# Gate and up products of the feed-forward layers with both parts of x as one moving operand of 512 columns

## What is computed

```python
def swiglu(h, w_gate, w_up, w_down):
    return (jax.nn.silu(h @ w_gate) * (h @ w_up)) @ w_down
...
    for i in range(DEPTH):
        mod = (c_act @ mod_w[i] + mod_b[i]).reshape(B, N_SUBLAYERS, 3, D)
        shift, scale, gate = mod[:, :, 0], mod[:, :, 1], mod[:, :, 2]
        h = modulate(rms_norm(x, norm_g[i, 0]), shift[:, 0], scale[:, 0])
        x = x + MACARON_WEIGHT * gate[:, 0, None, :] * swiglu(h, ffn_w_gate[i, 0], ffn_w_up[i, 0], ffn_w_down[i, 0])
        ...
        x = x + gate[:, 1, None, :] * y
        h = modulate(rms_norm(x, norm_g[i, 2]), shift[:, 2], scale[:, 2])
        x = x + MACARON_WEIGHT * gate[:, 2, None, :] * swiglu(h, ffn_w_gate[i, 1], ffn_w_up[i, 1], ffn_w_down[i, 1])
```

## Time and profile before

| | |
|---|---|
| time, median of 3 runs (lowest to highest) | 2218.18 us (2216.0 to 2218.39) |
| the profiled execution's own time | 2219.53 us |
| its span, first to last instruction | 2218.2 us |
| mean granted TensorE clock | 0.988 of full speed |
| PE busy | 2140.0 us, 96% of the span |
| DVE busy | 1497.4 us, 68% |
| ACT busy | 1082.5 us, 49% |
| GpSimd busy | 156.6 us, 7% |

### The profile page before, as it was taken

One profiled execution on the slowest core, in us unless ns is written; L12 is line 12 of the kernel. 1 busy time (PEld: TensorE's weight loads), 2 busy tenths in 40 slices (PEclk: granted clock), 3 DMA queues, 4 the chain that ended last, 5 costly groups with the idle time before them and its releaser, 6 DMA issues.

```text
span 2218.2 us, 33120 instructions
## 1 busy us (share of the span) xinstructions
PE 2140.0 (96%) x14096; PEld 1889.0 (85%) x14096; DVE 1497.4 (68%) x1960; ACT 1082.5 (49%) x1217; POOL 156.6 (7%) x192
## 2 busy tenths in 40 slices
PE   7999998999999999899999999999999999999998
PEld 5998765998899878687799887897998878988996
DVE  4677676877777786576655455568786655677874
ACT  4443565543444354555544346644554457444652
POOL 0311110111011100000000011100000111000000
PEclk9999998999999999999999999999999999999999
DMA  9977662987787855244355564435655564446651
GB/s 347 307 267 263 249 244 86 302 279 271 249 273 257 288 210 182 88 171 152 115 191 189 190 226 169 171 124 166 217 178 194 194 211 153 136 152 209 190 176 53
DMA packets 262818, 448.61 MB, mean 202 GB/s; under 512 B 11616, under 2 KB 147104, under 8 KB 262416
## 3 DMA queue, kind: packets, MB, share of 16 engines
q1 hardware_dynamic: 243616, 376.64, 50.2%
q0 software_dynamic: 18768, 68.75, 8.8%
q10 hardware_dynamic: 288, 1.11, 0.1%
HBM read 445.40 MB, written 1.06 MB: 201 GB/s over the span
## 4 chain that ended last, share of the span: by engine, by line
PE 88%; ACT 5%; DVE 5%; issue 1%; DMA 0%; SPq 0%; ACTq 0%; DVEq 0%
PE ps L1522 86%; ACT whi L1747 2%; DVE wlo L1952 1%; PE ps L1713 1%; PE ps L1680 1%; ACT S L1747 1%; ACT L1747 1%; ACT xhi L1747 1%; ACT xs L1747 0%; DVE S L2100 0%; DMA raw<-in_mod_w 0%; PE ps L1670 0%; DVE nbuf L2060 0%; ACT PT L1747 0%; PE ps L1630 0%
## 5 line engine op out<-in xcount | busy, mean ns | idle before, releaser
L1952 DVE TENSOR_TENSOR wlo<-raw,whi 128x2048 fp32r<-128x2048 f32 (+1 forms) x339 | 767.2, 2271 | 349.8 <-ACT whi L1747 349.3
L1747 ACT ACTIVATE whi<-raw 128x2048 fp32r<-128x2048 f32 (+1 forms) x339 | 640.7, 1895 | 363.6 <-PE ps L1522 343.7
L1522 PE MATMUL ps<-xhi,whi 128*128 128x256 f32 x2632 | 649.8, 287 | 6.4 <-DVE wlo L1952 4.4
L1522 PE MATMUL ps<-xhi,wlo 128*128 128x256 f32 x2632 | 643.5, 284 | 0.0
L1522 PEld LDWEIGHTS ps<-xhi,whi 128*128 128x128 f32 x2632 | 507.9, 193 | 11.7 <-issue 7.2
L1522 PEld LDWEIGHTS ps<-xhi,wlo 128*128 128x128 f32 x2632 | 508.0, 193 | 2.3 <-issue 2.0
L1522 PE MATMUL ps<-xlo,whi 128*128 128x256 f32 x2632 | 344.3, 283 | 0.1
L1522 PEld LDWEIGHTS ps<-xlo,whi 128*128 128x128 f32 x2632 | 327.6, 192 | 0.5 <-DVE xlo L2066 0.3
L1522 PE MATMUL ps<-whi,xhi 128*128 128x512 f32 x736 | 296.7, 403 | 13.5 <-DVE wlo L1952 10.5
L1522 PE MATMUL ps<-wlo,xhi 128*128 128x512 f32 x736 | 290.4, 395 | 0.0
L1522 PE MATMUL ps<-whi,hhi 128*128 128x512 f32 x528 | 210.0, 398 | 0.0
(11 more groups left out here) (234 smaller groups left out, 1966.7 us busy)
## 6 DMA issues: line engine op xcount, KB each, us to landing
raw<-in_w_in SPq DMA_DIRECT2D x52, 1024.0 KB, 4.9
raw<-in_ffn_w_gate SPq DMA_DIRECT2D x88, 512.0 KB, 4.6
raw<-in_ffn_w_up SPq DMA_DIRECT2D x88, 512.0 KB, 6.0
raw<-in_ffn_w_down SPq DMA_DIRECT2D x44, 1024.0 KB, 5.0
raw<-in_w_up SPq DMA_DIRECT2D x88, 512.0 KB, 4.8
raw<-in_dil_w_in SPq DMA_DIRECT2D x36, 1024.0 KB, 5.1
xs<-in_mod_w POOLq DMA_DIRECT2D x54, 512.0 KB, 6.2
nbuf<-in_mod_w POOLq DMA_DIRECT2D x46, 512.0 KB, 5.2
```

The lines of the kernel that those rows point to most:

```text
L1522: return nc.tensor.matmul(o, lhs, rhs, start=start, stop=stop, skip_group_check=True)
L1747: return nc.scalar.activation(o, i, func, **kw)
L1952: V.tensor_tensor(wlo[:, s["c"], 0:s["n"]], raw[:, s["slot"], 0:s["n"]], whi[:, s["c"], 0:s["n"]].bitcast(F32), ALU.subtract).then_inc(sem ...
```

## The change

Units 3 to 10 of each of the four layers (32 units of 44) are made in another form. `xhi` and `xlo` become two halves of one tile (`xhl` in the trace), so that one matmul can take both as a moving operand of 512 columns: `whi` by high x lands in the left half of a bank, `whi` by low x in the right half. `wlo` by high x stays a matmul of 256 columns into the left half. A unit has four output blocks, so it needs four banks; even units take G0 to G3, odd ones D0 to D3. Nothing on PE adds the halves any more. ACT copies the right halves to `e1` and `e2`, DVE adds the left halves from PSUM (two sums), ACT takes silu of `e1` in place, DVE multiplies, and the rest is as before. The turns of the modulation come between a unit's two pieces instead of behind the second, and take their bank from the four that the unit doesn't use.

```diff
-    def feature(self, src, need, nk=NC):
+    def feature(self, src, need, nk=NC, mid_turns=False):
...
+            if mid_turns and k0 == 0:
+                self.run_turns()
         self.x_read = tok
-        self.run_turns()
+        if not mid_turns:
+            self.run_turns()
...
     def gateup(self, q):
-        self.gateup_out(q, *self.feature("x", self.need_x))
+        if q < 3:
+            self.gateup_out(q, *self.feature("x", self.need_x, mid_turns=q == 2))
+        else:
+            self.gateup_wide(q)
+
+    def gateup_wide(self, q):
+
+        banks, self.idle_bank = ((G0, G1, G2, G3), D3) if q % 2 == 0 else ((D0, D1, D2, D3), G3)
+        bank_free = [self.free[b] for b in banks]
+        for k0 in (0, 4):
+            pc = self.take()
+            tok = self.ev("pe", "piece")
+            self.add("wide", banks=banks, k0=k0, c=pc["c"], w_lo=pc["w_lo"], need=[self.need_x(k0 + kk) for kk in range(4)],
+                     bank_free=bank_free if k0 == 0 else [])
+            self.used(pc, tok)
+            self.run_work()
+            if k0 == 0:
+                self.run_turns()
+        self.x_read = tok
+        s = q % 2
+        low = [self.ev("act", "low_out") for _ in range(2)]
+        gate = self.ev("dve", "wide_sum")
+        act = self.ev("act", "gate_act")
+        up = self.ev("dve", "wide_sum")
+        td = self.ev("dve", "hidden")
+        self.add("gateup_wide", s=s, banks=banks, piece=tok, e_free=self.e_free[s], low_out=low, gate=gate, gate_act=act, up=up)
+        self.free[banks[0]] = self.free[banks[1]] = gate
+        self.free[banks[2]] = self.free[banks[3]] = up
+        self.hidden_split(q, s, 1, td)
...
+                elif k == "wide":
...
+                        for m in range(4):
+                            w, v = vh[:, kk, m * P:(m + 1) * P], vl[:, kk, m * P:(m + 1) * P]
+                            mm(ps[:, s["banks"][m], :], w, xboth[:, :, kc, :], kc == 0, kc == NC - 1)
+                            ins = mm(ps[:, s["banks"][m], 0:T], v, xhi[:, kc, :], False, kc == NC - 1)
+                    ins.then_inc(sem["piece"])
...
+                elif k == "gateup_wide":
+                    q.wait_ge(s["piece"])
+                    q.wait_ge(s["e_free"])
+                    for e, b in ((e1, s["banks"][0]), (e2, s["banks"][2])):
+                        act(e[:, s["s"], :].rearrange("p (b n) -> p b n", b=2), ps[:, b:b + 2, T:2 * T],
+                            ACT.Copy).then_inc(sem["low_out"])
+                    q.wait_ge(s["gate"])
+                    act(e1[:, s["s"], :], e1[:, s["s"], :], ACT.Silu).then_inc(sem["gate_act"])
...
+                elif k == "gateup_wide":
+                    for e, b, low, n in ((e1, s["banks"][0], s["low_out"][0], 0), (e2, s["banks"][2], s["low_out"][1], 1)):
+                        q.wait_ge(low)
+                        o = e[:, s["s"], :].rearrange("p (b n) -> p b n", b=2)
+                        V.tensor_tensor(o, o, ps[:, b:b + 2, 0:T], ALU.add).then_inc(sem["wide_sum"])
+                    q.wait_ge(s["gate_act"])
+                    q.wait_ge(s["up"])
+                    V.tensor_tensor(e2[:, s["s"], :], e1[:, s["s"], :], e2[:, s["s"], :], ALU.mult).then_inc(sem["hidden"])
```

More of the change, by code:

```diff
@@ L32 @@
     "square", "moment", "var", "sqrt", "recip", "scaled", "x_turned", "x_hi", "x_full", "x_lo", "gate_mul", "resid",
-    "half", "gate_act", "hidden", "h_hi", "h_lo", "score", "biased", "expd", "weighed",
+    "half", "low_out", "wide_sum", "gate_act", "hidden", "h_hi", "h_lo", "score", "biased", "expd", "weighed",
     "turned", "pt", "value", "o_hi", "o_lo", "kept", "hn_sq", "hn_sum", "hn_sqrt", "hn_rec", "hn_mul", "hn_out",
@@ L73, in __init__ @@
         self.in_down = False
+        self.idle_bank = D3
         self.mod_ready = {}
@@ L310, in mod_part @@
             self.acc_turns.append([age or (2 if self.in_down else 1),
-                                   lambda: self.mod_turn(i, u, (G3 if self.in_down else D3) - u % 2, tok, acc)])
+                                   lambda: self.mod_turn(i, u, (G3 if self.in_down else self.idle_bank) - u % 2, tok, acc)])
     def mod_turn(self, i, u, bank, row, acc=None):
@@ L469, in down @@
             self.run_turns(age=False)
-            self.in_down = True
+            self.in_down, self.idle_bank = True, D3
             bank_free = [self.free[b] for b in (D0, D1, D2, D3)]
@@ L1363, in build @@
         nbuf = named("nbuf", [P, 4, T])
-        xhi = named("xhi", [P, NC, T], F32R)
-        xlo = named("xlo", [P, NC, T], F32R)
+        xboth = named("xhl", [P, 2, NC, T], F32R)
+        xhi, xlo = xboth[:, 0, :, :], xboth[:, 1, :, :]
         ident = named("ident", [P, P])
@@ L1560, in pe_program @@
                             ins = mm(place(m), vh[:, kk, m * P:(m + 1) * P], al[:, kc, :], False, kc == s["nk"] - 1)
+                    ins.then_inc(sem["piece"])
+                elif k == "wide":
+                    for t in s["bank_free"]:
+                        q.wait_ge(t)
+                    q.wait_ge(s["w_lo"])
+                    vh, vl = weights(s["c"], 4, 512)
+                    for kk in range(4):
+                        kc = s["k0"] + kk
+                        q.wait_ge(s["need"][kk][0])
+                        q.wait_ge(s["need"][kk][1])
+                        for m in range(4):
+                            w, v = vh[:, kk, m * P:(m + 1) * P], vl[:, kk, m * P:(m + 1) * P]
+                            mm(ps[:, s["banks"][m], :], w, xboth[:, :, kc, :], kc == 0, kc == NC - 1)
+                            ins = mm(ps[:, s["banks"][m], 0:T], v, xhi[:, kc, :], False, kc == NC - 1)
                     ins.then_inc(sem["piece"])
```

## The result

The changed kernel takes 2222.76 us (median of 20 runs, 2215.69 to 2227.84), the kernel before 2216.76 us in 20 runs of its own (2214.04 to 2221.57). The ratio is 1.0023, with a 95% interval of 1.0015 to 1.0031: about 5 us slower (3.3 to 6.9), at the edge of the 0.2% that the prediction calls no change. The runs of the change spread over 12.2 us, those of before over 7.5 us, and a longer run is mostly one with a lower clock: the four longest (2224.96 to 2227.84 us) have a mean granted clock of 0.984 to 0.987, the four shortest (2215.69 to 2219.07) one of 0.988 to 0.990.

A forecast was written before the change was run, and what follows sets the result against it. PE was taken to bound the kernel, with DVE's chain setting the pace in A to C after the change: 1.8 + 1.1 + 1.5 - 3.4 = +1.0 us, execution 2220.5 us, less 1.35 us for the median: 2219.2 us, range 2210 to 2225.5.

The forecast's parts named there:

- the prediction's own case: Wide units go at DVE's pace in layers A to C and PE's in D; 2214 to 2222 us, chance 0.52.
- within 0.2%: Whole kernel: no change a measurement can tell, under about 4.4 us either way; chance 0.57.
- PE's unit, 11.09 us: Wide feed-forward unit on PE: 32 x 0.2267 + 32 x 0.120 = 11.09 us, against 11.52 us before.
- That term of the sum: Layer D, without modulation parts, stays at PE's pace and keeps 8 x 0.43 = 3.4 us.
- DVE's round, 12.07 us: DVE's chain through one wide unit in layers with parts: 10.68 us grows by 1.39 us to 12.07 us.
- From unit 7 or 9 on PE goes at DVE's pace.: Wide units of A to C: DVE falls behind about 1 us a unit until PE must wait for it.
- The limit of 2.2 us: Wide units: DVE's lag at which PE first waits, for the bank a turn's result leaves 8.3 us into the round.
- The down phase is kept: First `wlo` behind the last sum to the last part's end stays as before: 48.38 us in C, 47.60 us in B.
- About 3 us at the last turn of A, B, C.: PE waits about 3 us for its last part at the last turn of each of these layers.
- The sum for A: Layer A, taken as the mean of B (1.1 us) and C (1.8 us): 1.5 us longer.
- The clock: Rival: the granted clock falls behind PE's waits at the last turns of A to C, 5.2 us, 2224.4 us; chance 0.13.
- three signs of being wrong: Down phase shorter by 2 us or more, late wide units' first sums under 11.8 us apart, or clock falling at last turns.

The follow-up runs named there:

- d_only: Wide form only in layer D, A to C narrow as in the kernel before: 2216.64 us, ratio 0.9994 to before.
- abc_only: Wide form only in layers A, B and C, D narrow as in the kernel before: 2224.37 us, ratio 1.0025 to before.
- contiguous: The changed kernel with the two parts of x side by side, so the 512 moving columns are one run of memory: 2223.24 us, ratio 1.0022 to before.

## Why the prediction was right in its number and wrong in a part

The prediction was 2219.2 us in a range of 2210.0 to 2225.5, and the measured median, 2222.76, lies inside. It lies outside the 2214 to 2222 us of the prediction's own case, and against before the forecast was +1.0 us where the ratio gives +5.1. The likeliest outcome was "within 0.2%" (0.57); it came out at that border, on the slower side, and the interval of the ratio doesn't tell which side of the border it is.

- **PE's unit, 11.09 us.** Right for seven of the thirteen units of A to C that have no turn; five take 11.31 us, and one in A, with a wait, 12.02. In D all take 11.31 us, so D keeps 1.7 us and not 3.4. That term of the sum was too large by 1.7 us. I took 0.2267 us from matmuls outside these layers; those of the down phase, in the same trace, start 0.233 us apart and give 11.31.
- **DVE's round, 12.07 us.** The step to the first `wlo` is 4.57 us (483.07 to 487.64), against 4.59. But two parts were charged with their busy time of 1.53 us, while the next instruction starts 1.45 us behind, twice a round. Over the seven rounds of layer C, first parts and results of turns included, the mean is 12.02 us (637.36 to 721.51), where the forecast's terms give 12.22. Late rounds are 11.6 and 12.5 us in turn.
- **"From unit 7 or 9 on PE goes at DVE's pace."** This failed. PE waits 0.65 us once in A, and nowhere over 0.15 us in the wide units of B and C. It finished unit 10 of C 92.59 us behind unit 2, against 95.61 us before, and had the whole gain in hand. Units with a turn take 12.0 us, so the lag grows more slowly than against 11.09 us. The limit of 2.2 us was wrong too: it is 11.09 - 8.3 us, less the usual 0.63, but the unit in question is the one with the turn. With 12.0 us the limit is 3.1 us, less what taking the result needs (0.15 to 0.7 us). In B and C the first sums in front of a unit with a turn come at most 3.1 us behind their unit's end, 2.5 beyond 0.63, and PE doesn't wait. In A they come 3.6 us behind it, at 129.48 us, and here it does (rows of DVE, then of PE):

```profile
136.27 1.53 DVE L2036 SCALAR_TENSOR_TENSOR xs<-nbuf,csil,xs 128x512 f32<-128x512 f32 x2
137.72 0.68 DVE L2044 TENSOR_TENSOR rows<-ps,rows 128x512 f32<-128x512 f32 x1
...
138.46 0.50 PE L1554 MATMUL ps<-xhl,whi 128*128 128x512 f32 x1 [0.65 <-DVE rows L2044]
```

- **The down phase is kept.** Right within what it varies. From the first `wlo` behind the last sum to the end of the last part: 49.0, 46.6 and 47.8 us in A, B and C, against 47.3, 47.6 and 48.4 us before. In `d_only`, whose A to C are in the order of before, it is 48.6, 49.1 and 49.6 us, so I carried over as fixed a term that differs by over 1 us between executions. With all kernels that keep the unchanged order it is 46.6 to 49.7 us.
- **"About 3 us at the last turn of A, B, C."** Right on the mean: nine waits in three executions of the wide form (the change, `abc_only`, `contiguous`) have a mean of 2.8 us.
- **The sum for A.** Wrong. I gave A the mean of B and C. But A has one turn fewer before the end of its unit 10, so before the change DVE entered its down phase 98.56 us behind unit 2 there and 99.43 us in B. With the change it is 101.31, 100.28 and 100.66 us in A, B and C: 2.7, 0.9 and 1.2 us later. The last turn starts 2.1, -0.5 and +0.4 us later than before, as means of the three executions, +2.0 us in all, where I had +4.4.
- **The clock.** This was a rival with 0.13, and it is the larger part of what is lost. Over the three executions the clock falls behind six of nine last turns. Counted from the start of the turn, since a lower clock costs nothing while PE waits, the time at the lower level takes 1.7, 6.1 and 4.5 us of PE's work, 4.1 us on the mean; the rival's price was 5.2 us. Its condition, two of the three waits, was met in two of the three executions and not in the change's own. The step that failed is its chance: I set one wait of 1.8 us with the clock at 1.00 against one of 1.9 us with 0.57 and took the fall for the exception. The sum with what was measured is 2.0 + 4.1 - 1.7 = 4.4 us. The layers' lengths in the three executions give +4.5 us as their mean, and the ratio 5.1.

Two of the prediction's three signs of being wrong showed: the clock fell at the last turns, and first sums of late wide units lay less than 11.8 us apart in every second round (697.40 to 709.02), though not on the mean. The errors had opposite signs: DVE's lag cost 2.4 us less than forecast, D gave 1.7 us less, and the clock took 4.1 us that my own case left out. That the range held is owed to the rivals in it and in part to luck; it doesn't make the likeliest case right.

## What to carry to other kernels

An engine that is busy 81% of a stage can still be the late one, if each of its rounds waits for another engine's answer; put work that depends on nothing into those waits before adding another exchange. A saving on the bounding engine that a later meeting point takes back can cost more than it saved, because the clock can be lower for the work behind the bounding engine's wait. And where executions differ by as much as the effect, compare the lengths of layers and the runs' ratio, not two spans.

## What the runs showed of the hardware

- **Behind waits of one length the clock can fall or stay.** At last turns the granted clock stayed at 1.00 behind waits of PE of 1.45, 2.25, 2.52 and 2.65 us, and fell behind 2.15, 2.61, 2.78, 3.39, 3.46, 3.69, 3.86 and 4.04 us. So waits of 2.15 to 2.65 us went either way, which may be why the change's runs spread wider; each kernel has one profile, so that isn't shown. The Trainium skill ("TensorE: Matmul & The Clock Gate", section "What's actually happening") says of a kernel's start that the number of slow matmuls varies from run to run. Whether it holds at these turns no run shows; what the traces show is that a fall cost 1.6 or 1.7 us of PE's work behind some turns and 2.8 to 3.1 us behind others.
- **The same 64 matmuls of a wide unit take 11.31 us before the first turn of a layer and 11.09 us after it**, and 11.31 us throughout D, which has no turn. Narrow units take 11.52 us everywhere. I didn't find the cause.
